# Delta heads: the order of the output's gate product, of half the system matrix, and of the last head's products

## The reference

```python
kk = jnp.einsum('bhcid,bhcjd->bhcij', kc, kc)
tri = jnp.where(strict, bc[..., :, None] * kk * decay, 0.0) + jnp.eye(CHUNK, dtype=f32)
sol = lax.linalg.triangular_solve(tri, rhs, left_side=True, lower=True, unit_diagonal=True)
def step(S, inp):                       # one chunk after the other
    v_new = u_c - jnp.einsum('bhid,bhde->bhie', w_c, S)
    o = jnp.einsum('bhid,bhde->bhie', qd_c, S) + jnp.einsum('bhij,bhje->bhie', qk_c, v_new)
    S = cd_c[..., None, None] * S + jnp.einsum('bhid,bhie->bhde', kd_c, v_new)
o = rmsnorm(o, o_norm_g) * jax.nn.silu(gate)
return o @ w_out
```

## Time and profile before

| | us |
|---|---|
| median of 3 executions | 2954.01 |
| lowest, highest | 2953.73, 2957.56 |
| the profiled execution, its own time | 2953.93 |
| its span in the profile | 2952.2 |
| TensorE busy in the span | 2902.3 |
| VectorE, ScalarE, GpSimd busy | 2131.2, 1257.9, 720.9 |
| mean granted TensorE clock, share of full speed | 0.996 |

### The profile page before, as it was taken

The page is one execution under the profiler, slowest core; times in us unless marked ns, Lnnn a source line. Parts: engine busy times, 40 slices in busy tenths (PEclk is TensorE's granted clock), DMA queues, the critical chain, the costliest instruction groups (busy, mean ns, idle before and its releaser), DMA issues.

```text
span 2952.2 us, 41363 instructions
## 1 busy us (share of the span) xinstructions
PE 2902.3 (98%) x14190; PEld 2409.8 (82%) x14190; DVE 2131.2 (72%) x2591; ACT 1257.9 (43%) x1857; POOL 720.9 (24%) x1126
## 2 busy tenths in 40 slices
PE   8999999999999999999899999999999999999998
PEld 7888887878888888887787788888887888878887
DVE  6665669858686868687886666666665667788887
ACT  4121124345454545455445454455453433344444
POOL 1000000014444444445001322222221356630000
PEclk9999999999999999999999999999999999999999
DMA  4213236332111211122532211111112344465542
GB/s 108 93 58 99 85 80 217 117 100 58 46 50 43 64 46 50 44 63 89 200 129 52 90 40 40 39 39 39 39 53 75 117 159 153 151 230 164 157 157 86
DMA packets 346911, 274.34 MB, mean 93 GB/s; under 512 B 82232, under 2 KB 297272, under 8 KB 342976
## 3 DMA queue, kind: packets, MB, share of 16 engines
q1 hardware_dynamic: 345664, 273.05, 30.1%
q10 hardware_dynamic: 1152, 0.07, 0.0%
HBM read 197.80 MB, written 75.27 MB: 92 GB/s over the span
## 4 chain that ended last, share of the span: by engine, by line
PE 89%; DVE 5%; issue 2%; DMA 1%; POOL 1%; ACT 1%; SPq 0%; DVEq 0%; POOLq 0%; ACTq 0%
PE banks L1105 9%; PE banks L1107 9%; PE banks L1106 9%; PE banks L1003 5%; PE banks L1005 5%; PE banks L1004 5%; PE banks L1087 3%; PE banks L1088 3%; PE banks L1089 3%; PE banks L1499 3%; PE banks L1500 3%; PE banks L1498 3%; PE banks L1590 3%; PE banks L1592 3%; PE banks L1591 3%; PE banks L1132 2%
## 5 line engine op out<-in xcount | busy, mean ns | idle before, releaser
L1105 PE MATMUL banks<-state_a_hi,weights_hi 128*128 128x512 f32 x1280 | 539.7, 422 | 0.9 <-DVE weights_lo L2221 0.8
L1107 PE MATMUL banks<-state_a_hi,weights_lo 128*128 128x512 f32 x1280 | 504.0, 394 | 0.0
L1106 PE MATMUL banks<-state_a_lo,weights_hi 128*128 128x512 f32 x1280 | 501.0, 391 | 0.0
L1107 PEld LDWEIGHTS banks<-state_a_hi,weights_lo 128*128 128x128 f32 x1280 | 240.3, 188 | 54.4
L1105 PEld LDWEIGHTS banks<-state_a_hi,weights_hi 128*128 128x128 f32 x1280 | 241.6, 189 | 39.5 <-issue 2.0
L1106 PEld LDWEIGHTS banks<-state_a_lo,weights_hi 128*128 128x128 f32 x1280 | 242.3, 189 | 34.0 <-issue 0.5
L831 POOL TENSOR_TENSOR beta<-beta,stick_left 128x128 f32<-128x128 f32 (+1 forms) x192 | 169.5, 883 | 393.0 <-DVE stick_left L2458 391.0
L2458 DVE TENSOR_TENSOR_SCAN stick_left<-stick_left,eps_column 128x128 f32<-128x128 f32 (+1 forms) x192 | 237.1, 1235 | 29.5 <-POOL beta L826 23.1
L2221 DVE TENSOR_TENSOR weights_lo<-weights_raw,weights_hi 128x1024 fp32r<-128x1024 f32 x133 | 180.6, 1358 | 80.6 <-ACT weights_hi L1618 68.2
L1618 ACT ACTIVATE weights_hi<-weights_raw 128x1024 fp32r<-128x1024 f32 x133 | 140.1, 1053 | 194.2 <-PE banks L1005 155.7
L1003 PE MATMUL banks<-state_a_hi,weights_hi 128*128 128x512 f32 x536 | 208.8, 389 | 1.5 <-DVE stream_again L2756 1.5
(11 more groups left out here) (532 smaller groups left out, 7327.8 us busy)
## 6 DMA issues: line engine op xcount, KB each, us to landing
weights_raw<-in_mlp_w_dram SPq DMA_DIRECT2D x34, 512.0 KB, 5.6
weights_raw<-in_gdn_w_in_dram SPq DMA_DIRECT2D x33, 512.0 KB, 4.1
weights_raw<-in_pool_w_in_dram SPq DMA_DIRECT2D x32, 512.0 KB, 4.1
state_a_lo<-relu_blocks_dram SPq DMA_DIRECT2D x16, 1024.0 KB, 7.1
weights_raw<-in_sb_w_in_dram SPq DMA_DIRECT2D x32, 512.0 KB, 4.1
relu_blocks_dram<-relu_sums SPq DMA_DIRECT2D x16, 1024.0 KB, 4.3
state_b_lo<-relu_blocks_dram SPq DMA_DIRECT2D x16, 1024.0 KB, 8.8
down_weights_raw<-in_mlp_w_dram SPq DMA_DIRECT2D x30, 512.0 KB, 5.3
```

What stands on the lines that cost most here:

```text
L1105: pe.matmul(psum[:, bank, :], whi, hi, start=(k == 0), stop=False)
L1106: pe.matmul(psum[:, bank, :], whi, lo, start=False, stop=False)
L1107: last = pe.matmul(psum[:, bank, :], wlo, hi, start=False, stop=(k == end - 1))
```

## The change

VectorE, all heads but the last: behind y1 it now does P1_4 of the next head (`level_step(LEVEL0)`) and only then y2; P1_4 of head 0 stands in front of the loop. y2 signals a semaphore of its own (`head_mixed`) instead of an event. The second half of the system matrix moves from fill step 15 to 17. Last head: head 0's output is rounded ahead of the first step, the products begin at hop 1 (42 products over 23 hops from hop 8), the remainders and roundings one step sooner. In `out2_tile` the sums of squares stand behind k = 3 of the first half instead of k = 5. Behind the last head VectorE splits one weight tile ahead of the last remainder, takes four chunks, splits the next tile, takes the fifth chunk and then makes five remainders.

```diff
-                    + [... + ["oT", "olo", "y1", "y2"])
+                    + [... + ["oT", "olo", "y1"])
@@ hops of the last head
-        OUT_K, OUT_FIRST, OUT_AT, OUT_HOPS = KC - 1, 2, 9, 22
+        OUT_K, OUT_FIRST, OUT_AT, OUT_HOPS = KC - 1, 1, 8, 23
@@ TensorE, out2_tile
-                            if h == 0 and k == 5:
+                            if h == 0 and k == 3:
                                 between()
@@ ScalarE, head
                     if kind == "last":
-                        if n == 0:
-                            act.wait_ge(bank_full, halves.value())
-                        if n == OUT_K - 1:
-                            act.wait_ge(*y2_of_head_6)
-                        if n < OUT_K:
-                            round_mixed(n)
+                        if n == OUT_K - 2:
+                            act.wait_ge(head_mixed, HEADS - 1)
+                        if n < OUT_K - 1:
+                            round_mixed(n + 1)
...
                 n = 0
+                if kind == "last":
+                    act.wait_ge(bank_full, halves.value())
+                    round_mixed(0)
...
-            ev.wait("dve", "y2")
+            act.wait_ge(head_mixed, HEADS)
             round_mixed(HEADS - 1)
@@ VectorE, head
+            def level_step(l):
+                ev.wait("pe", f"P{l}")
+                ev.did(f"P1_{l}", dve.tensor_tensor(P1[:, :, :], psum[:, 4, :].rearrange("p (c n) -> p c n", n=64),
+                                                   lmask[:, l - LEVEL0:l - LEVEL0 + 1, :].to_broadcast([P, TT, 64]), ALU.mult))
...
                     if kind == "last":
                         if n == 0:
                             stage_gate(kT, 1)
-                        if 0 < n <= OUT_K:
-                            rest_mixed(n - 1)
+                        if n < OUT_K:
+                            rest_mixed(n)
...
-                    if n in (13, 15):
-                        system((n - 13) // 2)
+                    if n in (13, 17):
+                        system((n - 13) // 4)
...
                 for l in range(LEVEL0, LEVELS):
                     w = 1 << l
-                    ev.wait("pe", f"P{l}")
-                    ev.did(f"P1_{l}", dve.tensor_tensor(...))
+                    if l > LEVEL0:
+                        level_step(l)
                     fill(n); n += 1
...
-                ev.wait("dve", "y1")
+                y1_done = ev.at("dve", "y1")
+                if kind != "last":
+                    ev.head = e + 1
+                    level_step(LEVEL0)
+                dve.wait_ge(*y1_done)
                 dve.wait_ge(stream_saved, 32)
                 yb = y_g[:, one(e), :].rearrange("p a n -> p (a n)")
-                ev.did("y2", dve.scalar_tensor_tensor(out=yb, ...))
-                ev.wait("dve", "y2")
+                dve.scalar_tensor_tensor(out=yb, ...).then_inc(head_mixed, 1)
+                dve.wait_ge(head_mixed, e + 1)
...
             rescale(2, KC)
+            level_step(LEVEL0)
@@ VectorE, behind the last head
+            split_weights()
             rest_mixed(HEADS - 1)
...
+            dve.wait_ge(stream_back[0], back[0].add(16))
+            for i in range(4):
+                take_chunk(i)
             split_weights()
-            dve.wait_ge(stream_back[0], back[0].add(16))
-            take_chunk(0)
-            split_weights()
-            next_rest(0)
-            for i in range(1, 5):
-                take_chunk(i)
-            for i in range(1, 5):
+            take_chunk(4)
+            for i in range(5):
                 next_rest(i)
                 if i == 2:
                     split_weights()
```

More of the change, by code:

```diff
@@ L251, in build @@
         yg_hi, yg_lo = sem("delta_y_hi"), sem("delta_y_lo")
+        head_mixed = sem("delta_head_mixed")
         block_hi, block_lo = sem("relu_sums_hi_done"), sem("relu_sums_lo_done")
@@ L263, in build @@
         DVE_MAIN = ([f"{x}{l}" for l in range(LEVEL0, LEVELS) for x in ("P1_", "X_")]
-                    + [f"{x}{c}" for c in range(TT) for x in ("R", "vw", "St") if (c or x != "R") and (c < TT - 1 or x != "St")] + ["oT", "olo", "y1", "y2"])
+                    + [f"{x}{c}" for c in range(TT) for x in ("R", "vw", "St") if (c or x != "R") and (c < TT - 1 or x != "St")] + ["oT", "olo", "y1"])
         ACT_MAIN = ["XT3", "vn", "XT4", "XT5", "osq", "ohi", "oln", "ors"]
@@ L2034, in _ @@
                 head("full")
-            ev.head = HEADS - 2
-            y2_of_head_6 = ev.at("dve", "y2")
             ev.head = HEADS - 1
             head("last")
-            ev.wait("dve", "y2")
+            act.wait_ge(head_mixed, HEADS)
             round_mixed(HEADS - 1)
@@ L2763, in rest_mixed @@
                 dve.tensor_tensor(A_lo[:, k, :], y_g[:, k, :], A_hi[:, k, :].bitcast(F32), ALU.subtract).then_inc(yg_lo, 1)
+            def level_step(l):
+                ev.wait("pe", f"P{l}")
+                ev.did(f"P1_{l}", dve.tensor_tensor(P1[:, :, :], psum[:, 4, :].rearrange("p (c n) -> p c n", n=64),
+                                                   lmask[:, l - LEVEL0:l - LEVEL0 + 1, :].to_broadcast([P, TT, 64]), ALU.mult))
             def head(kind, e):
-                ev.next[0] = 0
+                ev.next[0] = 1
                 col = lambda x, c: x[:, one(e), c:c + 1].rearrange("p a b -> p (a b)")
@@ L2809, in head @@
                     w = 1 << l
-                    ev.wait("pe", f"P{l}")
-                    ev.did(f"P1_{l}", dve.tensor_tensor(P1[:, :, :], psum[:, 4, :].rearrange("p (c n) -> p c n", n=64),
-                                                       lmask[:, l - LEVEL0:l - LEVEL0 + 1, :].to_broadcast([P, TT, 64]), ALU.mult))
+                    if l > LEVEL0:
+                        level_step(l)
                     fill(n); n += 1
@@ L2858, in head @@
                 sdn.add(4)
-                ev.wait("dve", "y1")
+                y1_done = ev.at("dve", "y1")
[3 more added lines that the diff above has]
+                dve.wait_ge(*y1_done)
                 dve.wait_ge(stream_saved, 32)
                 yb = y_g[:, one(e), :].rearrange("p a n -> p (a n)")
-                ev.did("y2", dve.scalar_tensor_tensor(out=yb, in0=flat(oT), scalar=o_gain[:, :], in1=(kT if kind == "last" else gT)[:, :], op0=ALU.mult, op1=ALU.mult))
-                ev.wait("dve", "y2")
+                dve.scalar_tensor_tensor(out=yb, in0=flat(oT), scalar=o_gain[:, :], in1=(kT if kind == "last" else gT)[:, :],
+                                         op0=ALU.mult, op1=ALU.mult).then_inc(head_mixed, 1)
+                dve.wait_ge(head_mixed, e + 1)
             normed_k()
```

## The result

The changed kernel takes 2966.91 us (median of 7 runs, 2961.53 to 2970.46) against 2954.63 for the kernel before in the same session (7 runs, 2953.73 to 2957.56): a ratio of 1.0037, 95% interval 1.0027 to 1.0047, so 12.3 us slower. The forecast was 2959.1, with +5.2 as its sum, and its range ended at 2967. So the result lies inside the range by 0.1 us, and that is luck: the range ended at rival A's time, and rival A is not what happened. By the bound of 5.9 us that the prediction set between same and slower, this is slower, the side that it gave 0.45 against 0.51. The sign was right, and the chain that was blamed; the price was more than twice what the sum said.

What follows compares the result with a forecast made beforehand. TensorE bounds the kernel (busy 2902.3 of 2952.2 us); NT1's later chain delays the next P4. Terms 5.6 + 1.5 - 0.6 - 1.4 + 0.1 = +5.2 on 2953.93 gave 2959.1 us, range 2951 to 2967.

Steps and rivals of the forecast that it cites:

- rival A: Tail of each head: GpSimd is caught by VectorE's weight remainder, 6 x 1.3 us more, 2967 us; chance 24%.
- What bounds the heads: Between heads: the chain from NT1 over GpSimd's inversion to the next P4 has 0.57 us to spare.
- P1_4 ahead of y2: Start of heads 1 to 7: P1_4 done first lets Q4 start sooner, 0.3 us of TensorE gained.
- NT1 behind St3 gives TensorE nothing: Chunk 3: vw3 and S3 come sooner, but chunk 4's weight remainder gives it back; NT1 ends 1.6 us later.
- Heads 1 to 6, +0.94 each: P4 to next P4: the later chain makes intervals 76.7 instead of 75.76 us, +5.6 us over six heads.
- Head 0 to head 1, +1.5: Already bound by the chain: NT1's shift of 1.6 us counts in full; +1.5 us, bounds +0.3 and +2.9.
- Last head and tail, -1.9: Last head and after: products from hop 1 -0.6, earlier sums of squares -1.4, order of chunks +0.1 us.
- The last remainder's 0.5: Tail: sums of squares two products earlier cut TensorE's 1.89 us wait for the last remainder, leaving 0.5 us.
- the order of the chunks, +0.1: Tail: the 1.54 us bank wait goes, but tile 5's weights are split later; 0.3 gained to 1.9 lost, +0.1 taken.
- Rival B: Heads: the chain hides a smaller NT1 delay of 0.6 us, P4 keeps its time; 2950.5 or 2947 us; chance 16%.
- rival C: Last head: tile 5's split meets GpSimd's sum for all of 3.42 us; +7.0, 2960.9 us; chance 10%.
- the rule weighed ahead of the result: Two-input VectorE work blocks GpSimd reads of SBUF, not writes: the memset passes, sum stays; otherwise some 8 us more.

Runs made afterwards that it cites:

- e1: The changed kernel with NT1 (second half of the system matrix) back at step 15; 2950.66 us, ratio 0.9990 to the kernel before.
- e2: The kernel before with NT1 alone moved to step 17, nothing else of the change; 2967.09 us, ratio 1.0048 to the kernel before.
- e6: The changed kernel with NT1 at step 16, ahead of that step's gate work; 2953.39 us, ratio 0.9994 to the kernel before.
- e3: Only the early first masked step (P1_4) of the change, the other four parts undone; 2953.51 us, ratio 0.9999 to the kernel before.
- e4: The kernel before with only the change's last-head and tail parts, new chunk order included; 2952.47 us, ratio 0.9993 to the kernel before.
- e8: The kernel before with the last head's products from hop 1 and earlier square sums, old chunk order; 2951.61 us, ratio 0.9991.
- e10: The changed kernel with NT1 one step later still, at step 18, behind the residual of chunk 4; 3013.02 us in one run.
- e9: The changed kernel with NT1 back at step 15 and 16 unread TensorE products ahead of head 0's P4; 2949.03 us, ratio 0.9981.
- e7: The changed kernel with NT1 at step 15, ahead of that step's convolution tap; 2953.59 us, ratio 0.9997 to the kernel before.
- e5: The changed kernel with 14 unread TensorE products before the wait for the inverse in each head but the first; 2975.99 us, one run.

## Why the prediction was right, and where its sum was off

- **What bounds the heads.** Right: the chain from NT1 over GpSimd to the next P4, with some half a microsecond to spare. e1 and e2 show it from both sides, and e6 measures the room: 0.4 us are free, and by the changed kernel not much more (1.7 later cost 1.1 to 1.25 us against e1's heads).
- **P1_4 ahead of y2.** Right in size: 0.3 to 0.45 us in each of heads 2 to 5 (e3), nothing where P4 is late (e2, which lacks it, has the changed kernel's 76.6 to 76.7 there).
- **NT1 behind St3 gives TensorE nothing.** Right. The 0.30 us ahead of S3 is gone in chunk 3 and comes back one chunk later, as a wait of vw4 behind the weight remainder: in the changed kernel the seven full heads have one wait each at L1413 for delta_v_new, 0.5 us at the longest, against the 0.3 of e1.
- **Heads 1 to 6, +0.94 each.** For heads 2 to 6 the steps held to the tenth, NT1's shift included (its end 44.70 us after P4, in e1 43.02: 1.7, with 1.6 taken); the cost was +0.64, 0.74, 0.87, 0.79 and 0.65, 3.7 where 4.7 was forecast. Of this 1.0, 0.6 is the mean of 75.76 with which the sum compared, where heads 2 to 5 had 75.9 before; 0.3 is head 6, which came out at 76.04 and not 76.7. Head 1 failed, for another reason.
- **Head 0 to head 1, +1.5.** The term that was undersized: it measured +3.9, outside its bounds of 0.3 and 2.9. The upper bound allowed for one step of GpSimd meeting a VectorE instruction. Two did, one after the other: the step behind a caught one was issued 0.35 us into VectorE's next instruction (1733.50 against 1733.15). That is rival A's mechanism, which the prediction placed in all heads but this one. What makes head 0 the first to be caught is the slow fetch: GpSimd starts 8.4 us after NT1's end there and 7.1 after it in heads 2 to 5, in the changed kernel as before.
- **The step that was missing.** A wait of TensorE was costed at its own length. Behind the 4.45 us in which TensorE did nothing its granted clock was 0.50 for the first 7.3 us of head 1, which made Q4 3.6 us late. The kernel before already showed it, at head 0: Q4 6.93 us after P4, and a granted clock of 0.52 from 1660.90 to 1667.00, behind a wait of 4.21 us. The prediction read head 0's end and not its start.
- **Last head and tail, -1.9.** Up to the 1000th product behind the last P4 they brought 2.6 us in e4 and 2.2 in e8, and 0.5 in the changed kernel, whose profile has the fall of the clock in the last head. That fall is in no term of the sum. The last remainder's 0.5 was right; the order of the chunks, +0.1, was a gain of 0.4.

In sum: forecast 5.6 + 1.5 - 1.9 = 5.2; measured 3.7 (heads 2 to 6) + 4.9 (head 1) + 3.9 (head 0) - 1.4 = 11.1, and 1.9 ahead of the first head that is taken for chance. The median of seven runs, +12.3, lies between. The total landed at rival A's 2967, but rival A as written, 1.3 us in each head, did not happen: it was one head caught, and one at half clock. That the total fell inside the range is luck, not the mechanism's doing. Rival B falls with e2, rival C with the 1.3 us at tile 5.

Of the rule weighed ahead of the result (the Trainium skill, SBUF — State Buffer, "Who interferes with whom"): the memset of the rows above ran from 1969.15 to 1969.27 beside a remainder that began at 1969.16 and lasted its 0.12 us, while L910 and L914, which read SBUF, were held to the end of the remainder they met. That a reader is held agrees with the rule. The memset, though, had begun first, by 0.01 us. The other side stands in the kernel before, outside the delta heads, where the prediction had found no row for it:

```profile
1375.12 1.82 DVE L2221 TENSOR_TENSOR weights_lo<-weights_raw,weights_hi 128x1024 fp32r<-128x1024 f32 x1
1376.02 0.10 POOL L841 MEMSET stick_left<- 128x1 f32 x1 [0.15 <-POOL beta L831]
```

This memset was issued 0.9 us into a remainder that ran for another 0.9, and took 0.10 us: a step that only writes was not held, as the rule says.

## What to carry to other kernels

When a chain runs beside a full engine, measure its room in both directions before moving its first link: here 0.4 us were free, 1.7 cost 1.2 a head, and the next step, with a neighbour caught and the clock lost, cost 8. A wait on TensorE is not worth its length alone: look in the granted clock of the stretch behind each wait that the kernel already has, and price a new long one with what the old one cost. And compare the granted clock of every stretch before calling a difference between two profiles the work of an edit: the last head lost up to 2 us by it in some kernels and not in others. Where such a wait cannot be shortened, even unread products in it can pay: 16 of them took 3.5 us off head 0 in the profile here.

## What the runs showed of the hardware

The same 16 products of 128x64 took 1.90 to 2.00 us at a granted clock of 1.00 and 3.67 us behind a wait of 4.45 us, at 0.50; the 128x512 products were issued every 0.23 and every 0.43 us. The waits behind which the clock was at the lower level for some of the next stretch were not only the ones over 4 us: in e2, e8 and e10 TensorE waited 2.77, 2.57 and 2.87 us ahead of head 0, and P4 to Q4 took 5.73, 5.73 and 5.71 us, between the 4.01 of e9 without a wait and the 6.7 to 7.2 behind waits of over 4 us in the same place; in e7 a wait of 2.99 us was followed by 7.22. Behind the waits of 0.4 to 1.1 us Q4 came 4.0 to 4.1 us after P4, at full clock; but in the last head the clock fell in six of the profiles with no wait over 1.21 us in the 5.5 us ahead, so the length of the one wait before does not settle it. By the Trainium skill, TensorE: Matmul & The Clock Gate, "What's actually happening", the clock is a gate that activity opens and idleness closes between these two levels; the filled gaps of e5 and e9 agree.

That a GpSimd step caught by a VectorE instruction can be followed by a second one, caught by the next, was seen in each head of e10 and in head 0 of the changed kernel, of e2 and of e5 (0.99 to 1.23 us each against 0.23 free). Not tried: moving the weight remainder off GpSimd's tail, which might make NT1's new place free; and real products in head 0's gap instead of unread ones.
